# Value chunks of a Gated DeltaNet stage: transposed on TensorE, or by VectorE in 32x32 blocks with a trip through DRAM

## The chip, the cores and the metric

One core of a Trainium2 chip runs the whole kernel. The metric is the time of one execution in device microseconds. The profile is of one execution of its own.

## The reference

The input is 256 tokens of width 1024. Two layers of a first block (windowed attention, gated linear attention and attention into a memory) are followed by two layers of feed-forward, mixer, feed-forward. The mixer of the last layer is the Gated DeltaNet, the stage that is changed:

```
proj = x @ w_in                       # 1024 -> q 1024, k 1024, v 2048, z 2048, beta 16, a 16
qkv  = silu(causal_depthwise_conv(qkv, conv_w))     # width 4, along the tokens, one filter for each channel
q, k = l2norm(q), l2norm(k)           # 8 heads of 128, each used by 2 value heads
o    = chunk_gated_delta_rule(q, k, v, g, beta)     # 16 value heads of 128
o    = rms_norm(o) * norm_w * silu(z)
out  = o @ w_out
```

## The kernel before

The tokens lie in two tiles of 128 (TT = 2). Weights arrive in units of 1 MB in a ring of four slots (SyncE issues the loads), ScalarE rounds each unit to w_hi (steps `hi:n:half`, L209), VectorE forms the rest w_lo (`lo:n:half`, L227), and TensorE multiplies each tile three times (L245 to L247), 24 matmuls of 128x512 for a unit. A unit may start when both halves of its w_lo are there.

In the Gated DeltaNet stage the projection comes in chunks of 512 columns: k0, ba (beta and a), k1, q0, q1, v0 to v3, z0 to z3, of two units each (ba is one small one). The k0 units are numbers 0 and 1; v0 has 9 and 10, v1 11 and 12, v2 13 and 14, v3 15 and 16, z0 17 and 18, z1 19 and 20. What each engine does, and in which order, is written out by hand in GDN_ORDER. Every engine walks the same list and does its own part of each step, so moving a step moves it in the order of each engine that has a part in it; between engines only semaphores order anything. `unit:v1:0:3` is quarter 3 of the first unit of chunk v1.

After a chunk's two units, ScalarE copies the two banks A[0] and A[1] to the chunk buffer u (`evac`, L2557), with the tokens in the partitions. The convolution runs along the tokens, so the channels must be in the partitions. `conv:c:part` does this for half a chunk: TensorE makes four 128x128 transposes from u into bank A[2] or A[3] (L2362), ScalarE writes the last tap's product to t (L2605), and VectorE adds the other three taps with six operations that read the bank (L2781). Steps `silu` follow on both engines, then for k and q `l2` and `norm` (a matmul with ones, L2370), for v `vt` (four transposes back, L2405, and the copy to v). The banks A[2] and A[3] are shared by conv, norm, vt, qk, kk and ba, in the order of the list. Two chunk buffers alternate, and the squares of `z2` go through net.tmp.

Steps `core:g:x` are the delta rule for two value heads. In x2, x1 and x0 a triangular inverse is put together from 16x16 blocks; p0 to p4 apply it. The blocks themselves are inverted on GpSimd (`gather`, function solve, L2191 and L2193), once for the first half and once for the second. SyncE brings them there and back through DRAM: `blocks`, `gather`, `solved` and `spread`, the last with 15 small DMAs that core x2 waits for. GpSimd has nothing else to do in this stage but three loads at its start.

Of the kernel before, what the change touches and what calls it, by code (L numbers as in the profile page):

```python
# [1707 lines left out]
class Conv:  # L1708
# [1403 lines left out]
```

## Time and profile before

| | |
|---|---|
| median of 3 runs | 1417.77 us (1417.53 to 1418.01) |
| the profiled execution | 1416.56 us, span 1414.8 us |
| TensorE busy | 1392.3 us, 98% |
| VectorE busy | 1026.2 us, 73% |
| ScalarE busy | 1011.9 us, 72% |
| GpSimd busy | 68.9 us, 5% |
| DMA queue of SyncE | 233.57 MB, 51.1% of the 16 DMA engines' span |
| DMA queue of GpSimd | 3.35 MB, 0.8% |

The stage runs from about 957 us to about 1224 us of the span. A share over the whole span says little of it: the engines are read stage by stage. A matmul's end is modelled, and the next one starts before it, so on TensorE one reads the distance from one start to the next (about 0.23 us for a 128x512 matmul), and not the durations.

### The profile page before, as it was taken

The numbers are of one execution on the slowest core, as the hardware profiler recorded it, in microseconds if no ns is written. First come the engines' busy times: TensorE is split into PE (matmuls) and PEld (weight loads), VectorE is DVE, ScalarE is ACT, GpSimd is POOL, SyncE is SP. The second block draws the span as 40 slices with busy tenths as digits, with TensorE's granted clock in tenths as the row PEclk, the third lists the DMA queues.
The fourth block names the chain that finished last, engine by engine and source line by source line (L and its number), as shares of the span: only waits on it lengthen the run. The fifth ranks groups of instructions, "written<-read, shape, count | busy, mean of one in ns | idle before, by whom it ended". The sixth has DMA issues, their size and how long they took to land.

```text
span 1414.8 us, 20634 instructions
## 1 busy us (share of the span) xinstructions
PE 1392.3 (98%) x7859; PEld 1142.9 (81%) x7859; DVE 1026.2 (73%) x1417; ACT 1011.9 (72%) x1826; POOL 68.9 (5%) x163
## 2 busy tenths in 40 slices
PE   6999999999999999999999999999999999999998
PEld 5888888888888887788887888887778888788886
DVE  5878788777666766676667766677989886876665
ACT  7657574748777554587875977767888886588784
POOL 8000000000000000000000000001030300000000
PEclk9999999999999999999999999999999999999999
DMA  7542453345656555565655565646453432566562
GB/s 234 166 142 91 145 200 121 119 149 180 201 186 206 180 190 181 158 207 188 205 181 179 195 202 185 203 157 194 129 163 112 118 123 90 165 208 200 187 206 91
DMA packets 168291, 238.27 MB, mean 168 GB/s; under 512 B 21554, under 2 KB 114640, under 8 KB 168192
## 3 DMA queue, kind: packets, MB, share of 16 engines
q1 hardware_dynamic: 166496, 233.57, 51.1%
q0 software_dynamic: 1632, 3.35, 0.8%
q8 instruction: 63, 1.03, 0.3%
q14 instruction: 36, 0.29, 0.1%
q10 hardware_dynamic: 64, 0.02, 0.0%
HBM read 235.07 MB, written 1.84 MB: 167 GB/s over the span
## 4 chain that ended last, share of the span: by engine, by line
PE 93%; ACT 3%; DVE 2%; DMA 1%; issue 1%; SPq 0%; DVEq 0%; ACTq 0%
PE A L245 17%; PE A L246 17%; PE A L247 17%; PE M L247 5%; PE G L246 5%; PE M L246 5%; PE G L247 5%; PE M L245 5%; PE G L245 5%; PE A L1325 1%; PE G L1246 1%; PE G L1293 1%; DVE tmp L414 1%; PE M L1303 1%; ACT w_hi L209 1%; DVE x_lo L419 1%
## 5 line engine op out<-in xcount | busy, mean ns | idle before, releaser
L227 DVE TENSOR_TENSOR w_lo<-raw,w_hi 128x1024 fp32r<-128x1024 f32 (+2 forms) x296 | 506.8, 1726 | 128.7 <-ACT w_hi L209 128.0
L209 ACT ACTIVATE w_hi<-raw 128x1024 fp32r<-128x1024 f32 (+2 forms) x296 | 426.7, 1462 | 120.9 <-DMA raw<-in_ffn_w_gate_up 93.3
L245 PE MATMUL A<-w_hi,x_hi 128*128 128x512 f32 (+1 forms) x640 | 258.7, 404 | 3.6 <-DVE x_lo L419 1.0
L247 PE MATMUL A<-w_hi,x_lo 128*128 128x512 f32 (+1 forms) x640 | 247.1, 386 | 0.0
L246 PE MATMUL A<-w_lo,x_hi 128*128 128x512 f32 (+1 forms) x640 | 246.5, 385 | 0.0
L690 ACT ACTIVATE ffn_ffn_hT<-ffn_ffn_hb 32x128 f32<-32x128 f32 x576 | 176.9, 307 | 15.6 <-DVE ffn_ffn_hb L755 2.5
L245 PEld LDWEIGHTS A<-w_hi,x_hi 128*128 128x128 f32 x640 | 120.2, 188 | 33.5 <-DVE x_lo L419 6.8
L247 PEld LDWEIGHTS A<-w_hi,x_lo 128*128 128x128 f32 x640 | 120.1, 188 | 25.1
L245 PE MATMUL A<-w_hi,ffn_ffn_hT_hi 128*128 128x512 f32 x352 | 139.0, 395 | 0.0
L246 PE MATMUL A<-w_lo,ffn_ffn_hT_hi 128*128 128x512 f32 x352 | 138.4, 393 | 0.0
L246 PEld LDWEIGHTS A<-w_lo,x_hi 128*128 128x128 f32 x640 | 120.5, 188 | 21.0 <-issue 0.7
L247 PE MATMUL A<-w_hi,ffn_ffn_hT_lo 128*128 128x512 f32 x352 | 136.9, 389 | 0.0
L247 PE MATMUL M<-w_hi,x_lo 128*128 128x512 f32 x320 | 124.5, 389 | 0.0
L245 PE MATMUL G<-w_hi,x_hi 128*128 128x512 f32 x320 | 124.5, 389 | 0.0
L246 PE MATMUL G<-w_lo,x_hi 128*128 128x512 f32 x320 | 124.5, 389 | 0.0
L245 PE MATMUL M<-w_hi,x_hi 128*128 128x512 f32 x320 | 124.5, 389 | 0.0
L246 PE MATMUL M<-w_lo,x_hi 128*128 128x512 f32 x320 | 124.5, 389 | 0.0
L247 PE MATMUL G<-w_hi,x_lo 128*128 128x512 f32 x320 | 124.5, 389 | 0.0
L247 PEld LDWEIGHTS A<-w_hi,ffn_ffn_hT_lo 128*128 128x128 f32 x352 | 66.1, 188 | 14.9
L245 PEld LDWEIGHTS A<-w_hi,ffn_ffn_hT_hi 128*128 128x128 f32 x352 | 66.1, 188 | 14.6
L246 PEld LDWEIGHTS A<-w_lo,ffn_ffn_hT_hi 128*128 128x128 f32 x352 | 66.2, 188 | 13.0
L245 PEld LDWEIGHTS G<-w_hi,x_hi 128*128 128x128 f32 x320 | 60.1, 188 | 12.6
(392 smaller groups left out, 2018.5 us busy)
## 6 DMA issues: line engine op xcount, KB each, us to landing
raw<-in_ffn_w_gate_up SPq DMA_DIRECT2D x176, 512.0 KB, 4.8
raw<-in_ffn_w_down SPq DMA_DIRECT2D x88, 512.0 KB, 4.0
raw<-in_w_in SPq DMA_DIRECT2D x48, 512.0 KB, 4.2
raw<-in_gdn_w_in SPq DMA_DIRECT2D x48, 512.0 KB, 4.6
raw<-in_sc_w_in SPq DMA_DIRECT2D x24, 512.0 KB, 4.3
raw<-in_w_out SPq DMA_DIRECT2D x16, 512.0 KB, 4.5
raw<-in_gdn_w_out SPq DMA_DIRECT2D x16, 512.0 KB, 4.0
raw<-in_w_mem_kv SPq DMA_DIRECT2D x8, 512.0 KB, 5.9
```

Of the source, the lines that this page charges most:

```text
L209: ins = act.activation(net.w_hi[:, v % RING, part], net.raw[:, v % RING, part], ACT.Copy)
L227: ins = dve.tensor_tensor(net.w_lo[:, v % RING, part], net.raw[:, v % RING, part], net.w_hi[:, v % RING, part].bitcast(F32), ALU.subtract)
L245: pe.matmul(out, xh, hi[:, k, c, :], start=start and k == 0, stop=False)
L246: pe.matmul(out, xh, lo[:, k, c, :], start=False, stop=False)
L247: mm = pe.matmul(out, xl, hi[:, k, c, :], start=False, stop=stop and k == nk - 1)
L414: dve.tensor_tensor(self.y(n), self.banks[n][:, :].rearrange("p (k t) -> p k t", k=4), self.g[:, 4 * h:4 * h + 4].unsqueeze(2).to_broadcas ...
L419: dve.tensor_tensor(self.part(self.x_lo, n), self.y(n), self.part(self.x_hi, n).bitcast(F32), ALU.subtract).then_inc(self.lo.sem, 1)
L690: ins = act.activation(self.hT[32 * b:32 * b + 32, :, :, i, :].rearrange("p k t n -> p t k n"), self.hb[32 * i:32 * i + 32, :, :, b, :], A ...
L1246: mm = pe.matmul(bank[:, n * P + t * 64:n * P + (t + 1) * 64], self.KE[rows, 1 + lev, tok], right, start=True, stop=True, tile_position=(D ...
L1293: mm = pe.matmul(bank[:, at:at + keys], qT[rows, pair, tt * P:(tt + 1) * P], kT[rows, pair, 0:keys], start=True, stop=True, tile_position= ...
L1303: mm = pe.transpose(bank[:, b * P:(b + 1) * P], self.Pb[:, i % 3, b * P:(b + 1) * P], ident[:, :])
L1325: mm = pe.matmul(O[:, tt * T + at:tt * T + at + HD], pt[:, b * P:(b + 1) * P], v[:, kt, cols], start=(kt == 0), stop=(b == blocks[tt][-1]))
```

## The change

The value chunks v0 to v3 are no longer transposed by TensorE. ScalarE's evac writes them with the columns in another order. In a new step `tb` VectorE transposes the chunk in place in 32x32 blocks, one instruction of 128x1024. GpSimd's queue then writes the 512 KB to DRAM, waits for it, and in step `mv` reads it back with four DMAs, one for each block row; their runs are of 32 floats (128 bytes), 1024 runs for each DMA. The chunk then has its channels in the partitions, in SBUF, and ScalarE and VectorE read it there in place of a bank. A third chunk buffer is made from net.tmp (v0 and v3 use it), and the squares of `z2` go to net.scratch. Where an evac reuses a buffer that held a value chunk, it waits for that chunk's last reader. GDN_ORDER is written anew around this.

```
-    unit:v1:0:1 hi:14:0 solved:0
-    unit:v1:0:2 hi:14:1
-    unit:v1:0:3 silu:q1:0:0 kk:4:0
+    unit:v1:0:1 solved:0
+    unit:v1:0:2 hi:14:0 hi:14:1
+    unit:v1:0:3 tb:v0 mv:v0 evac:v1:0 silu:q1:0:0 kk:4:0
     unit:v1:1:0 lo:13:0
-    unit:v1:1:1 evac:v1:0 spread:0 kk:4:1 lo:13:1
+    unit:v1:1:1 spread:0 kk:4:1 lo:13:1
     unit:v1:1:2 kd:4:0
     unit:v1:1:3 kd:4:1 evac:v1:1
-    unit:v2:0:0 silu:q1:1:0 silu:q1:0:1 l2:q1:0 lo:14:0 kk:5:0
-    unit:v2:0:1 silu:q1:1:1 kk:5:1 kd:5:0
-    unit:v2:0:2 l2:q1:1 kd:5:1 lo:14:1 lo:15:0 lo:15:1 hi:15:0
-    unit:v2:0:3 hi:15:1 norm:q1:0 norm:q1:1
-    unit:v2:1:0 core:0:x2 core:1:x2 core:0:t2 core:1:t2
+    unit:v2:0:0 silu:q1:1:0 silu:q1:0:1 lo:14:0 kk:5:0
+    unit:v2:0:1 tb:v1 silu:q1:1:1 kk:5:1 kd:5:0
+    unit:v2:0:2 l2:q1:0 l2:q1:1 kd:5:1 lo:14:1 lo:15:0 hi:15:0 lo:15:1
+    unit:v2:0:3 mv:v1 hi:15:1 core:1:x2 norm:q1:0 norm:q1:1
+    unit:v2:1:0 core:0:x2 core:0:t2 core:1:t2
...
-    unit:k1:1:3 lo:6:0 hi:6:1 evac:k1:1 norm:k0:0
-    unit:q0:0:0 lo:6:1 l2:k0:1 conv:k1:0
-    unit:q0:0:1 hi:7:0 norm:k0:1 hi:7:1
+    unit:k1:1:3 ba:0 lo:6:0 hi:6:1 norm:k0:0 evac:k1:1
+    unit:q0:0:0 lo:6:1 l2:k0:1
+    unit:q0:0:1 conv:k1:0 hi:7:0 norm:k0:1 hi:7:1
...
-    unit:q1:1:3 lo:9:0 lo:9:1 lo:10:0 lo:10:1 hi:10:1 ba:2 norm:k1:0 blocks:0 norm:k1:1 conv:q0:0 conv:q0:1
+    unit:q1:1:2 l2:k1:1 lo:9:0 lo:9:1 lo:10:0 lo:10:1 hi:10:1 ba:2 norm:k1:0 blocks:0 evac:q1:0
+    unit:q1:1:3 norm:k1:1 conv:q0:0 conv:q0:1
...
+    unit:v3:0:1 silu:v0:0:0 tb:v2 silu:v0:1:0 qk:0
+    unit:v3:0:2 core:1:t1 mv:v2
...
+    unit:z0:0:2 tb:v3
+    unit:z0:0:3 mv:v3 core:0:p4 vt:v1:0
...
+BY_BLOCKS = ("v0", "v1", "v2", "v3")
+U_OF = {"k0": 0, "k1": 1, "q0": 0, "q1": 1, "v0": 2, "v1": 0, "v2": 1, "v3": 2, "z0": 0, "z1": 1, "z2": 0, "z3": 1}
...
+            elif step[0] == "tb":
+                n = self.bys.index(step[1])
+                pool.wait_ge(*self.u_blocks(n + 1))
+                pool.dma_start(self.u_dram[n], self.turned(step[1]).rearrange("p k n -> p (k n)"))\
+                  .then_inc(self.u_out.sem, 16)
+            elif step[0] == "mv":
+                n = self.bys.index(step[1])
+                pool.wait_ge(*self.u_out(16 * (n + 1)))
+                src = self.u_dram[n].rearrange("(i c) (m b n) -> b c m i n", i=4, b=4, n=32)
+                for b in range(4):
+                    pool.dma_start(self.turned(step[1])[32 * b:32 * b + 32, :, :]
+                                 .rearrange("p k (t i n) -> p (k t) i n", t=TT, i=4), src[b]).then_inc(self.u_in.sem, 16)
...
-            elif kind == "conv":
+            elif kind == "conv" and step[1] not in BY_BLOCKS:
                 c, part = step[1], int(step[2])
                 bank = self.take(pe, step)
                 pe.wait_ge(*self.evacuated(2 * self.evacs.index(c) + 2))
...
+            elif kind == "tb":
+                c = step[1]
+                u = self.turned(c).rearrange("p k n -> p (k n)")
+                dve.wait_ge(*self.evacuated(2 * self.evacs.index(c) + 2))
+                dve.transpose(u, u).then_inc(self.u_blocks.sem, 1)
```

The step `conv:v0:0` stays at `unit:v2:1:1`, `conv:v1:0` at `unit:v3:0:3`, `conv:v2:0` at `unit:z0:1:0` and `conv:v3:0` at `unit:z1:0:3`; ScalarE waits there for the data to have landed from DRAM.

## Rows read from the trace of the kernel before

**Rows 1.** The page's busy times, and its chain that ended last, by engine
```profile
PE 1392.3 (98%) x7859; PEld 1142.9 (81%) x7859; DVE 1026.2 (73%) x1417; ACT 1011.9 (72%) x1826; POOL 68.9 (5%) x163
...
PE 93%; ACT 3%; DVE 2%; DMA 1%; issue 1%; SPq 0%; DVEq 0%; ACTq 0%
```

**Rows 2.** Windows of the stage: length, engines' busy times, clock, DMA share, GB/s
```profile
1037.00:1050.00 13.00, 13.00 (x67) 10.86 (x66) 12.01 (x29) 10.29 (x18) 1.30 (x4) 1.00 0.59 129
1050.00:1072.00 22.00, 21.84 (x364) 17.18 (x363) 18.06 (x40) 17.25 (x37) 0.00 (x0) 1.00 0.48 155
1072.00:1112.00 40.00, 40.00 (x468) 34.02 (x467) 36.32 (x84) 33.26 (x75) 3.18 (x5) 1.00 0.40 119
```

**Rows 3.** TensorE's timeline around conv:v0 and conv:v3:1: start, duration, engine, line
```profile
1057.34 0.60 PE L2362 MATMUL A<-ident,gdn_gd_u 128*128 128x128 f32 x4
1057.87 0.69 PE L2476 MATMUL G<-gdn_gd_T,gdn_gd_MT 32*32 32x32 f32 x32
1058.49 0.66 PE L2362 MATMUL A<-ident,gdn_gd_u 128*128 128x128 f32 x4
1058.90 0.47 PE L245 MATMUL A<-w_hi,x_hi 128*128 128x512 f32 x1
1059.22 0.39 PE L246 MATMUL A<-w_lo,x_hi 128*128 128x512 f32 x1
...
1113.07 0.60 PE L2362 MATMUL A<-ident,gdn_gd_u 128*128 128x128 f32 x4
1113.60 1.14 PE L2491 MATMUL G<-gdn_gd_T,gdn_gd_MT 64*64 64x64 f32 x16
```

**Rows 4.** TensorE's timeline at conv:k1:0 and at conv:q0:1
```profile
987.72 0.40 PE L247 MATMUL A<-w_hi,x_lo 128*128 128x512 f32 x1
988.22 0.66 PE L2362 MATMUL A<-ident,gdn_gd_u 128*128 128x128 f32 x4
...
1017.97 0.66 PE L2362 MATMUL A<-ident,gdn_gd_u 128*128 128x128 f32 x4 [0.49 <-ACT gdn_gd_sg L2622]
```

**Rows 5.** VectorE's groups by shape in the stage: busy us, mean ns
```profile
L2781 DVE SCALAR_TENSOR_TENSOR gdn_gd_t<-A,cols,gdn_gd_t 128x254 f32<-128x254 f32 x32 | 13.9, 477 | 0.6
...
L2862 DVE TENSOR_TENSOR gdn_gd_u<-gdn_gd_u,gdn_gd_sg 128x1024 f32<-128x1024 f32 x4 | 4.9, 1218 | 0.0
...
L755 DVE STREAM_TRANSPOSE ffn_ffn_hb<-ffn_ffn_h 128x512 f32<-128x512 f32 x1 | 0.7, 712 | 0.0
```

**Rows 6.** Timeline: lo:14:1, first matmul of unit 14, first value tap
```profile
1049.71 1.22 DVE L227 TENSOR_TENSOR w_lo<-raw,w_hi 128x1024 fp32r<-128x1024 f32 x1
...
1051.99 0.79 PE L245 MATMUL A<-w_hi,x_hi 128*128 128x512 f32 x1
...
1058.00 0.84 ACT L2605 ACTIVATE gdn_gd_t<-A,cols 128x256 f32<-128x256 f32 x2
```

**Rows 7.** GpSimd's DMA instructions by shape (8 rows; 128 rows of 512 bytes)
```profile
L3025 POOL DMA_DIRECT2D rows<-in_norm_g x6 | 3.0, 502 | 0.0
...
L3025 POOL DMA_DIRECT2D rows<-in_gdn_conv_w x1 | 0.6, 556 | 0.0
```

**Rows 8.** DMA issues: count, KB each, median us from issue to landing
```profile
brow<-in_norm_g POOLq DMA_DIRECT2D x6, 512.0 KB, 3.9
...
gdn_gd_MT<-gdn_solved SPq DMA_DIRECT2D x16, 16.0 KB, 2.6
```

**Rows 9.** DMA queue between 1044 and 1050 us: packets, MB, share of 16 engines
```profile
q1 hardware_dynamic: 2365, 0.24, 36.7%
```

**Rows 10.** GpSimd's timeline: one operation of each solve
```profile
1028.00 1.17 POOL L2191 TENSOR_TENSOR gdn_gd_Dpart<-gdn_gd_D,gdn_gd_Dinv 128x64 f32<-128x64 f32 x1
...
1115.69 0.31 POOL L2191 TENSOR_TENSOR gdn_gd_Dpart<-gdn_gd_D,gdn_gd_Dinv 128x64 f32<-128x64 f32 x1
```

**Rows 11.** Timeline: last DMA of the second spread, and core:4:x2 behind it
```profile
1132.66 0.45 SPq L2256 DMA_DIRECT2D gdn_gd_MT<-gdn_solved  x1
...
1137.86 0.73 PE L2457 MATMUL G<-gdn_gd_T,gdn_gd_MT 32*32 32x16 f32 x64
```

More of the change, by code:

```diff
@@ L1970 @@
-    unit:v3:0:1
-    unit:v3:0:2
-    unit:v3:0:3 lo:16:0 core:1:x0 core:0:x0 hi:17:1 silu:v0:0:1 lo:16:1 vt:v0:0 silu:v0:1:1 core:1:t0 lo:17:0 ba:3
+    unit:v2:0:0 silu:q1:1:0 silu:q1:0:1 lo:14:0 kk:5:0
[3 more added lines that the diff above has]
+    unit:v2:1:0 core:0:x2 core:0:t2 core:1:t2
+    unit:v2:1:1 conv:v0:0 core:0:x1 hi:16:0 conv:v0:1 evac:v2:0 core:1:x1 hi:16:1
@@ L1984 @@
+    unit:z0:0:3 mv:v3 core:0:p4 vt:v1:0
+    unit:z0:1:0 vt:v1:1 z2:z0:0 core:1:p4 lo:19:1 conv:v2:0 hi:20:1 core:2:x2
     unit:z0:1:1 conv:v2:1 blocks:1 evac:z0:0
-    unit:z0:1:2 hi:21:0 evac:z0:1
+    unit:z0:1:2 evac:z0:1 hi:21:0
     unit:z0:1:3 hi:21:1 core:3:x2 silu:v2:0:0 core:2:t2
-    unit:z1:0:0
-    unit:z1:0:1 silu:v2:1:0 lo:20:0 silu:v2:0:1
+    unit:z1:0:0 silu:v2:1:0
+    unit:z1:0:1 lo:20:0 silu:v2:0:1
     unit:z1:0:2 core:3:t2
@@ L2022 @@
     out:2:1 lo:28:1
[L2023 to L2024 removed]
+    out:2:2 hi:29:1 hi:30:0 lo:29:0 hi:30:1 core:6:p1 core:7:p1 core:6:p2 core:7:p2
+    out:2:3 z1:z3:0
     out:3:0 core:7:p3 core:6:p3
@@ L2061, in __init__ @@
         self.evacuated = s("evacuated")
+        self.u_blocks, self.u_out, self.u_in, self.u_read = (s(f"u_{n}") for n in ("blocks", "out", "in", "read"))
+        self.u_dram = net.scratch_dram(f"{name}_u", [len(BY_BLOCKS), P, TT * 512])
         self.ba = {x: s(f"ba_{x}") for x in ("act", "dve", "pe")}
@@ L2095, in __init__ @@
         self.silus = [x[1:3] for x in self.steps if x[0] == "silu" and x[3] == "0"]
+        self.bys = [x[1] for x in self.steps if x[0] == "tb"]
+        self.convs = [x[1:3] for x in self.steps if x[0] == "conv" and x[1] in BY_BLOCKS]
         self.norms = [x for x in self.steps if x[0] == "norm"]
@@ L2098, in __init__ @@
         self.l2s = [x[1:3] for x in self.steps if x[0] == "l2"]
-        uses = [x for x in self.steps if x[0] in ("conv", "norm", "vt", "qk", "kk") or
+        uses = [x for x in self.steps if x[0] == "conv" and x[1] not in BY_BLOCKS or x[0] in ("norm", "vt", "qk", "kk") or
                 (x[0] == "ba" and x[1] in "t12") or (x[0] == "ot" and int(x[1]) < 4)]
@@ L2109, in u_of, with turned, conv_read @@
     def u_of(self, c):
-        return self.u[:, [x for x in self.evacs if x != "ba"].index(c) % 2]
+        return self.us[U_OF[c]]
+    def turned(self, c):
+        return self.u_of(c).rearrange("p t c -> p (t c)").rearrange("p (k n) -> p k n", k=4)
+    def conv_read(self, eng, c, part):
+        if c in BY_BLOCKS:
+            eng.wait_ge(*self.u_read(self.convs.index((c, part)) + 1))
+        else:
+            eng.wait_ge(*self.bank_dve[int(part)](self.reads(("conv", c, part))))
     def tensors(self, net):
@@ L2594, in act @@
                 c, part = step[1], int(step[2])
-                bank = self.written(act, step)
+                if c in BY_BLOCKS:
+                    act.wait_ge(*self.u_in(64 * (self.bys.index(c) + 1)))
+                    u = self.turned(c)[:, 2 * part:2 * part + 2, :]
+                else:
+                    u = self.written(act, step)[:, :].rearrange("p (k n) -> p k n", k=2)
                 n = self.silus.index((c, step[2]))
@@ L2793, in dve @@
                 if step[3] == "0":
-                    taps = ("conv",) + step[1:3]
-                    dve.wait_ge(*self.bank_dve[int(step[2])](self.reads(taps)))
+                    self.conv_read(dve, step[1], step[2])
                     if n >= 2 and self.silus[n - 2][0][0] != "v":
```

107 lines of the change are left out of this document (57 added, 50 removed).

## The prediction

> **What bounds the kernel now.** I read the page first: TensorE is busy 98% of the span and holds 93% of the chain that ended last [rows 1]. VectorE's 73% there is a mean over all stages, so I went on to the windows of the stretch that the change touches. There TensorE has next to no idle time, while VectorE is busy 12.01 of 13 us, 18.06 of 22 and 36.32 of 40 [rows 2]. The reader is to see two things. A microsecond taken from TensorE is a microsecond won as long as nothing else is late. And VectorE has only 0.99 + 3.94 + 3.68 = 8.6 us free in these 75, so it is the next bound. The DMA engines are busy 0.40 to 0.59 of the time [rows 2], and GpSimd nearly idle. Last I read the timelines around each step that moves.
>
> **What TensorE loses.** Eight steps conv:v go, four transposes each. The first holds the engine from 1057.34 to 1057.87, 0.53 us. The second from 1058.49 to 1058.90, 0.41 us, and the weight matmul behind it then takes 0.32 us to the next start in place of 0.23, so a change between the two kinds of work costs 0.09. The last one takes 0.53 us [rows 3]. Over the eight, by the same reading, the blocks hold 0.36 to 0.53 us and add up to 3.56 us, with 0.09 more where weight matmuls stand on both sides. Against that, where a conv stood between weights and a core step, the change of kind stays and moves to that step: I give back about 0.1 us at two or three places. The sum is 3.4 us. Its bounds are 8 x 0.36 = 2.9 and 8 x 0.53 = 4.2 us.
>
> **What the new sequence does early.** conv:k1:0 now stands one quarter later, behind norm:k0:0 and unit:q0:0:1, and evac:k1:1 has that much more time. Before, 0.50 us lay between the last matmul and its transposes where 0.23 is usual [rows 4]; that is 0.27 us won. norm:k1:0 moves ahead of unit:q1:1:3, so ScalarE reads the bank of norm:k1:1 without the other norm in front, and conv:q0:1, which waited 0.49 us [rows 4], waits less; I take 0.3 us, between 0 and 0.5. Together 0.6 us.
>
> **What VectorE gains in work.** A block transpose of 128x512 takes 0.712 us, and an operation with one output of 128x1024 takes 1.218 [rows 5]. I take 1.22 us for a tb, between 1.2 and 2 x 0.712 = 1.42. Four are 4.9 us. The 48 tap operations now read SBUF in place of a bank; at 477 ns for 254 elements against 1218/4 = 305 at the least for a quarter of 1024 [rows 5] they could get faster, up to 8 us in all, or stay. The fixed part of so short an operation speaks for staying: I take 0. ScalarE's taps and its evac in another column order I take at 0 too, and ScalarE has 13 - 10.29 = 2.7 us of cover just where evac:v1:0 moves ahead of silu:q1:0:0 and makes it wait for TensorE [rows 2].
>
> **Where that is not hidden.** tb:v0 and tb:v1 both come ahead of lo:14:1 in VectorE's order, and that step ended at 1050.93 for a unit that started at 1051.99 [rows 6]: a margin of 1.06 us. The two add 2.44 us. VectorE's idle time between 1037 and 1050 is 0.99 us [rows 2]; if 0.8 of it absorbs, lo:14:1 ends at 1052.6 and unit 14 waits 0.6 us (bounds 0 and 1.4). Queued behind it on VectorE are lo:15, the norms of q1 and the t2 of core 0 and 1, for which TensorE's x1 waits; the moved conv:v0 has cleared TensorE's way by less than that, and these just meet. From there to unit 20 tb:v2 and tb:v3 follow, and TensorE comes up to 3 us early for the t2 and t1 of core 2 and 3, the vt of v2 and lo:20:1, while VectorE has 7.6 us idle to give [rows 2], much of it waits for TensorE's transposes that now fall away. I take another 0.6 us there, with bounds 0 and 1.8. Sum of stalls 1.2 us.
>
> **The round trip.** tb:v0 can begin where conv:q1 ends on VectorE, about 1039.1, and ends at 1040.3. The write of 512 KB on GpSimd's queue is like the row of brow, 3.9 us from issue to landing [rows 8]: 1044.3. Then four DMAs of 1024 runs. The trace has none of this size on that queue. An issue of 8 rows takes 0.502 us and one of 128 rows 0.556 [rows 7]. By the difference, 0.45 ns for each further run, one of 1024 takes 0.96 us and the four 3.8; in plain proportion it takes 8 x 0.556 = 4.4 and the four 17.8. I take the first, as 16 times the rows cost only a tenth more, and keep both. The transfer: between 1044 and 1050 the packets were mostly 64 byte ones and 2365 of them took 36.7% of 6 us on 16 engines, 14.9 ns each [rows 9]. 4096 of them are 61 us on 16 engines, 3.8 us, much of it beside the issuing. With 2.6 us for the last to land [rows 8] the chunk is there at about 1050.7, and at 1055 if the spread of the first half and two weight units, which fall into this stretch, halve its speed. The first tap stood at 1058.00 [rows 6]. So v0 has 3 to 7 us to spare, and the three later ones 20 us or more from tb to tap. Weight loads meet 1 MB more for each value chunk and 3.8 us of small packets; in the windows they share engines that are half idle [rows 2], and a unit is loaded a few us ahead of its rounding: 0.
>
> The Trainium skill, page "VectorE: DVE Perf Modes", section "The three transpose paths", speaks against this part: a plain DMA that transposes by its access pattern is said to be 19 times slower than the crossbar's when the innermost stride of the destination is large. Here both sides have runs of 32 floats and the elements are turned before, so the sum above stays; by that rule the chunk would come late and the time would be that of the rival "data late". No row here shows such a copy.
>
> The third buffer adds waits of evac v2, v3, z0 and z1 for conv steps that lie ten or more quarters back: 0. The new wait before the squares is for VectorE's own reduction just before: 0.
>
> **The sum.** 3.4 + 0.6 - 1.2 = 2.8 us less. The profiled execution took 1416.56 us (span 1414.8 and 1.8 around it), which is 1.2 under the median; I take the difference over to the median: 1417.77 - 2.8 = 1415.0 us.
>
> **Rivals.** *VectorE has slack for all of it*: the tap operations do get shorter, or its idle time absorbs the four tb whole. Then no stall: 3.4 + 0.6 = 4.0 us less, 1413.8. For it speak 8.6 us of idle for 4.9 us of work, against it that the margin of unit 14 is 1.06 us.
>
> *VectorE becomes the bound*: none of its idle time can be used, because it lies between semaphores. Then 4.9 us of work less the margin of 1.06 comes out on TensorE, 3.8 against 4.0 won: 1417.6. For it speaks that 92% of a window is already full [rows 2].
>
> *Data late*, the one on the other side: GpSimd's descriptors take their time in proportion to runs. A chunk then holds GpSimd's queue for 3.9 + 0.5 + 17.8 = 22.2 us, and four in a row end at 1040.3 + 88.8 + 2.6 = 1131.7, where conv:v3 stood at 1113. ScalarE, whose rounding of weights is queued behind the tap, stops; after some 5 us of units in hand TensorE stops too. 19 - 5 - 4 = 10 us slower: 1428. It decides from the point where the four DMAs together hold the queue for more than 1058 - 1044.3 - 2.6 = 11 us; at 14 us the gain is gone. The Trainium skill, page "SBUF — State Buffer", section "SBUF: two separate sides", gives a way to it: descriptors of GpSimd's DMAs are written through a port pair that VectorE holds in its faster modes. No row here shows it for a DMA.
>
> *The second solve is late*: a GpSimd operation took 1.17 us beside VectorE's w_lo and 0.31 us beside conv:v3 [rows 10]. conv:v3 now has two inputs in SBUF; if each of its twelve operations holds up one of GpSimd's, the solve ends 12 x (0.477 - 0.39) = 1 us later, up to 5 if it is shut out whole. The last DMA of the second spread was issued at 1132.66 and takes 2.6 us, and core:4:x2 came at 1137.86 [rows 11]: 2.6 us of margin. So 0, and at the worst 2.4 us lost: 1417.4. The same page, section "Who interferes with whom", says that a VectorE operation with two SBUF inputs holds up a GpSimd one that reads SBUF; the 1.17 us agree.
>
> **Chances.** The forecast 0.45 (1414.2 to 1416), slack for all 0.18 (1413.2 to 1414.2), VectorE or the solve as bound 0.22 (1416 to 1418.5), data late 0.15 (1419 to 1435). The range: below, the second case with TensorE's upper bound of 4.2, so 1413.0; above, past the third case and into the weaker half of the last, 1419.0. Leaving out all but a tenth at the top and little below holds 8 in 10. 0.2% is 2.8 us, about what measurement tells from none, and the forecast lies on that line: its half and the second case make faster 0.42; its other half and most of the third same 0.42; slower 0.16.
>
> **What would show it.** Right: no L2362 with a value chunk and 32 fewer of them, TensorE's idle in the stage under 2 us, four block transposes of about 1.22 us, the reads landed by 1055 for v0, GpSimd's four issues about 1 us each. Wrong: issues of several us; ScalarE's tap idle for a DMA; TensorE idle ahead of unit 14 or of x1 and t1 for VectorE by more than 2 us in all; weights (L209) waiting for DMA; the second solve ending after core:4:x2 is due. The forecast fails most likely through VectorE's order, next through GpSimd's queue.

## The result: slower by 0.38%, outside the range

The changed kernel takes 1422.29 us (median of 9 runs, 1420.18 to 1425.88), the kernel before, run beside it, 1417.53 (9 runs, 1416.38 to 1418.14). The ratio is 1.0038, interval 1.0029 to 1.0047. I had forecast 1415.0 and given 0.16 to "slower". The profiled execution of after took 1421.78 us, its span 1420.0.

**The page of after**, busy times and the chain by engine:

```profile
PE 1392.2 (98%) x7827; PEld 1141.7 (80%) x7827; DVE 1032.3 (73%) x1421; ACT 1012.1 (71%) x1826; POOL 90.9 (6%) x183
...
PE 87%; DVE 3%; DMA 2%; POOL 2%; ACT 2%; SPq 1%; issue 1%; DVEq 0%; ACTq 0%; POOLq 0%
```

TensorE has its 32 matmuls fewer, as planned. VectorE has 6.1 us more work, where 4.9 was planned. TensorE's share of the chain fell from 93 to 87% [rows 1]; GpSimd and SP's queue stand in it now, and DMA has 2% for 1%: the chain runs over transfers.

**Windows of after**, laid 1.8 us later, as the stage starts that much later. Columns as in [rows 2]:

```profile
1038.80:1051.80 13.00, 13.00 (x66) 10.78 (x65) 12.48 (x25) 8.61 (x16) 5.54 (x10) 1.00 0.73 182
1051.80:1073.80 22.00, 19.99 (x333) 14.75 (x333) 18.97 (x44) 17.39 (x36) 5.26 (x8) 1.00 0.76 228
1073.80:1113.80 40.00, 39.19 (x469) 33.17 (x468) 39.16 (x87) 34.38 (x75) 10.49 (x13) 1.00 0.64 163
```

TensorE is idle 2.0 us of the middle window, where it was 0.16 before, and the DMA engines' share is 0.76 where it was 0.48 [rows 2].

**What TensorE waited for**, 957 to 1250 us, after (line, releaser, us in total, times, longest):

```profile
PE G L2487 <- DMA gdn_gd_MT<-gdn_solved: 3.3, 2, 1.7
PE M L2499 <- issue: 1.1, 1, 1.1
PE A L280 <- ACT gdn_gd_u L2596: 0.8, 1, 0.8
PE G L2506 <- DVE gdn_gd_T L2964: 0.6, 1, 0.6
```

L2487 is step x2, the first to read a spread's matrices. It waits twice, once for each spread; before, it never did. L2499 is the second half of t2 and waits for no semaphore ("issue"). L280 was there before. VectorE, which I had feared, stands fourth.

**TensorE's timeline of after** at both spreads and in t2 (the bracket is the idle time before, and what ended it):

```profile
1054.24 0.44 PE L2487 MATMUL G<-gdn_gd_T,gdn_gd_MT 32*32 32x16 f32 x32 [1.57 <-DMA gdn_gd_MT<-gdn_solved]
...
1141.52 0.73 PE L2487 MATMUL G<-gdn_gd_T,gdn_gd_MT 32*32 32x16 f32 x64 [1.73 <-DMA gdn_gd_MT<-gdn_solved]
...
1145.37 0.23 PE L2499 MATMUL M<-gdn_gd_MT,gdn_gd_X 32*16 32x16 f32 x9
1146.72 0.32 PE L2499 MATMUL M<-gdn_gd_MT,gdn_gd_X 32*16 32x16 f32 x21 [1.12 <-issue]
```

core:4:x2 comes at 1141.52, where it came at 1137.86 [rows 11]. The last row shows a step broken in two: nine matmuls, 1.12 us of nothing, twenty-one more.

**The second solve and what follows it, after**: GpSimd's reads of v3, its first and last operation, SP's last transfer of the spread:

```profile
1104.63 4.02 POOL L2231 DMA_DIRECT2D tmp<-gdn_u  x4 [6.24 <-DMA gdn_u<-tmp]
...
1112.28 0.39 POOL L2209 TENSOR_TENSOR gdn_gd_Dpart<-gdn_gd_D,gdn_gd_Dinv 128x15 f32<-128x15 f32 x1 [2.94 <-DMA gdn_gd_D<-gdn_blocks]
...
1129.57 1.50 POOL L2216 COPY gdn_gd_D<-gdn_gd_Dinv 128x256 f32<-128x256 f32 x1
...
1139.62 0.45 SPq L2286 DMA_DIRECT2D gdn_gd_MT<-gdn_solved  x1
```

The last transfer is issued 7.0 us later than before [rows 11]. In the trace of before the solve began at 1108.51 and ended with its copy at 1124.05; here it is 1112.28 and 1131.07. So 3.8 us are a late start and 3.2 a longer solve, 1.8 of the former being the later start of the stage.

**When the matrices land and when they are wanted.** I subtract from each time the start of the stage (TensorE's first wait of 0.78 us, at 969.59 before and 971.36 after). The last matrix of the first spread then lands at 80.3 us before and 82.8 after, and the step that reads it is due at 84.3 before; in the new order it is due at 81.2 (e1, where it waits for nothing). So the transfer lands 2.5 us later and its reader comes 3.1 us sooner. The last matrix of the second spread lands at 164.8 before and 170.1 after. Its own transfer is as quick as ever (1.75 and 1.85 us); what is late there is the solve.

**How I compare the stage.** The offset between two executions at entry is not the stage's doing, so I take the *stage time*: from matmul 1300 to matmul 1500 of L245, counted from 0 (1012.17 to 1229.24 before). It is 217.1 us before and 220.2 after. Summed start to start by kind of matmul, the transposes of `gdn_gd_u` in it fall from 5.82 to 1.98 us. So 3.84 us came off and 3.1 + 3.84 = 6.9 came on. Of the 3.84, 3.55 are the value chunks; the other 0.29 is a shorter wait of conv:q0:1. The stage time is of one profiled execution of each kernel, and after and after again differ by 0.4 us in it.

### The profile page after: what moved, and what is told of

Its sections match the earlier page's. It is cut to its first block, busy times and chain, and to the rows that moved or that the text cites. A ratio compares the mean times of both kernels' runs of the same rounds, so it can differ in the third digit from the quotient of the medians.

```text
span 1420.0 us, 20597 instructions
## 1 busy us (share of the span) xinstructions
PE 1392.2 (98%) x7827; PEld 1141.7 (80%) x7827; DVE 1032.3 (73%) x1421; ACT 1012.1 (71%) x1826; POOL 90.9 (6%) x183
## 4 chain that ended last, share of the span: by engine, by line
PE 87%; DVE 3%; DMA 2%; POOL 2%; ACT 2%; SPq 1%; issue 1%; DVEq 0%; ACTq 0%; POOLq 0%
PE A L245 16%; PE A L246 15%; PE A L247 15%; PE M L245 5%; PE M L247 5%; PE G L246 5%; PE G L245 5%; PE G L247 5%; PE M L246 5%; PE A L1325 1%; POOL gdn_gd_Dinv L2211 1%; PE G L1246 1%; POOL gdn_gd_Dpart L2209 1%; DMA gdn_gd_D<-gdn_blocks 1%; PE G L1293 1%
## 5 line engine op out<-in xcount | busy, mean ns | idle before, releaser
L245 PE MATMUL A<-w_hi,x_hi 128*128 128x512 f32 (+1 forms) x640 | 259.6, 406 | 3.5 <-DVE x_lo L419 1.2
L245 PEld LDWEIGHTS A<-w_hi,x_hi 128*128 128x128 f32 x640 | 120.7, 189 | 33.7 <-DVE x_lo L419 6.8
L245 PE MATMUL A<-w_hi,ffn_ffn_hT_hi 128*128 128x512 f32 x352 | 139.1, 395 | 0.0
L245 PE MATMUL G<-w_hi,x_hi 128*128 128x512 f32 x320 | 124.5, 389 | 0.0
L245 PE MATMUL M<-w_hi,x_hi 128*128 128x512 f32 x320 | 124.5, 389 | 0.0
L245 PEld LDWEIGHTS A<-w_hi,ffn_ffn_hT_hi 128*128 128x128 f32 x352 | 66.1, 188 | 14.3
L245 PEld LDWEIGHTS G<-w_hi,x_hi 128*128 128x128 f32 x320 | 60.1, 188 | 12.6
```

What stands on the lines that cost most here:

```text
L245: pe.matmul(out, xh, hi[:, k, c, :], start=start and k == 0, stop=False)
```

## The experiments

Medians are compared by ratio, as chips differ (the kernel before ran at 1417.1 to 1418.8 beside these). The granted clock is the share of full speed that TensorE was given. "Clock" is what the stage lost to one under 1.00: (1 - clock) times the length, summed over its windows. Taking it off is an estimate, right as far as TensorE was busy meanwhile.

| kernel | median us | ratio (95%) | stage us | of it clock |
|---|---|---|---|---|
| before | 1417.5 | 1 | 217.1 | 0 |
| after | 1422.3 | 1.0038 (1.0029-1.0047) | 220.2 | 0 |
| after again (e14) | 1423.8 | 1.0042 (1.0027-1.0058) | 220.6 | 0 |
| e1 new order, TensorE turns all | 1419.8 | 1.0012 (1.0003-1.0022) | 219.2 | 0 |
| e2 old order, four turned | 1421.7 | 1.0011 (0.9997-1.0025) | 221.1 | 1.7 |
| e3 after without its transfers | 1416.8 | 0.9989 (0.9980-0.9999) | 215.6 | 0 |
| e4 after, v3 by TensorE | 1419.7 | 1.0015 (1.0005-1.0025) | 219.9 | 1.7 |
| e17 after, v0 by TensorE | 1421.3 | 1.0020 (1.0011-1.0030) | 221.1 | 1.7 |
| e10 after, v0 and v3 by TensorE | 1418.4 | 1.0004 (0.9996-1.0013) | 217.0 | 0 |
| e9 after without block transposes | 1423.2 | 1.0036 (1.0024-1.0048) | 222.0 | 3.4 |
| e5 core:1:x2 back | 1422.4 | 1.0034 (1.0023-1.0045) | 221.2 | 1.7 |
| e6 cores 4, 5 later | 1425.1 | 1.0051 (1.0039-1.0063) | 224.4 | 3.4 |
| e7 both | 1429.0 | 1.0074 (1.0061-1.0086) | 227.0 | 8.5 |
| e11 old order, v1 late, v2 | 1422.8 | 1.0037 (1.0023-1.0051) | 221.1 | 1.7 |
| e12 the same and v0 | 1421.8 | 1.0032 (1.0019-1.0045) | 219.9 | 1.7 |
| e15 old order, v1 early, v2 | 1416.2 | 0.9983 (0.9975-0.9992) | 214.9 | 0 |
| e19 the same and v0 | 1416.1 | 0.9985 (0.9977-0.9994) | 216.1 | 0 |
| e20 the same and v0, v3 | 1419.5 | 1.0008 (0.9999-1.0017) | 218.7 | 1.7 |
| e16 stream moved by 256 | 1426.0 | 1.0052 (1.0039-1.0064) | 228.2 | 5.1 |
| e18 stream moved by 128 | 1425.0 | 1.0051 (1.0038-1.0063) | 222.5 | 1.7 |

### The order, the turning and the transfers apart: e1, e2, e3, e9

```diff
 e1: -BY_BLOCKS = ("v0", "v1", "v2", "v3")     +BY_BLOCKS = ()       (no tb, no mv)
 e2: the order of before, with tb:v0 mv:v0 at v1:0:0, v1 at v1:1:3, v2 at v2:1:2, v3 at z0:0:2
 e3: -act.wait_ge(*self.u_in(...))             +act.wait_ge(*self.u_blocks(n + 1))    (no write, no reads)
 e9: no dve.transpose; pool.wait_ge(*self.evacuated(...)) before the write
```

e3 leaves the values between blocks unturned and e9 the values inside them, so their outputs are not the reference's.

> The new sequence of steps and the three chunk buffers alone: TensorE transposes the value chunks as before, no block transposes and no trip to DRAM. Theory A (the time goes into two waits of TensorE for the spreads of the solved blocks, because the second solve starts late and runs long and because core:1:x2 was moved ahead): without the DMAs of the chunks and with the taps read from a bank the solve takes 15.5 us again and both spreads land in time, so about 1417.5, within 1 of the kernel before. Rival B (VectorE has become the bound): also near 1417.5, since its 4.9 us are gone. Rival C (the new sequence itself is the loss, whatever turns the chunks): 1420 or more.

> The old sequence of steps, with block transposes and the trip to DRAM put in right behind each value chunk's evac. Theory A: core:1:x2 stands where it stood and waits less, by about 1.5 us; the second spread is as late as in the changed kernel; 1420 to 1421. Rival B: VectorE's order is not fitted to the 4.9 us, TensorE waits for it in many places, 1423 or more. Rival C: 1418 or less, as the loss was in the sequence.

> The changed kernel without the writes and reads of the chunks: VectorE transposes the 32x32 blocks, and the taps read them as they lie, so blocks stay out of place and the values are not the reference's. VectorE and ScalarE do all that they do in the changed kernel. Theory A: the first wait (about 1.8 us) goes, blocks and gather of the second half are not held up (about 3 us of 7), the solve stays long: 1417 to 1419. Rival B: the DMAs cost nothing, 1421 to 1422. Rival C: 1421 to 1422.

> The changed kernel without the four block transposes of VectorE (the values of v are then not the reference's); writes, reads and their waits stay and start 1.2 us earlier. Theory A (the DMA round trip and its effect on the spreads and the second solve are the loss): within 0.7 us of the changed kernel, 1421.5, with the gaps at core:1:x2 and core:4:x2 still over 1.2 us each. Rival B (VectorE's 4.9 us are the loss): 2 us or more faster than the changed kernel, and the two gaps small.

e1: the order alone is no gain; it costs 2.1 us of stage, with TensorE turning the values. By kind of matmul it is spread: 0.7 us behind weight matmuls, 0.6 at x1 and x2, 0.5 at the transposes of v, 0.4 at the products of v, less 0.3 won at the norms. It had been written for a kernel whose values VectorE turns.

e3: without the transfers, VectorE's four block transposes and the new order included, the stage is 215.6 us, 4.6 below after and 3.6 below e1. The value transposes that e1 has and e3 has not hold TensorE for 3.8 us, so VectorE's 4.9 us of added work cost about 0.2. The stage thus adds up: 2.1 for the order, 3.6 off for turning on VectorE, 4.6 for the transfers, 3.1 in all. No x2 waits in e3. Its waits of TensorE, first and third row:

```profile
PE A L280 <- ACT gdn_gd_u L2584: 0.8, 1, 0.8
...
PE M L2487 <- issue: 0.6, 1, 0.6
```

e9 is the mirror of it: transfers without VectorE's 4.9 us. By its median it is as slow as after; less the clock its stage is 222.0 - 3.4 = 218.6 us, so that VectorE's transposes account for 1.6 us at most. In e2 core:1:x2 does not wait, core:4:x2 waits 1.75 us, and t2 and t1 stall; less the clock its stage is 219.4. Its ten runs go from 1415.5 to 1422.8 us, four of them below the median of the kernel before, 1418.7 beside it, so one profile says little of it.

### Which chunk: e4, e17, e10

```diff
 e4:  BY_BLOCKS = ("v0", "v1", "v2")     e17: BY_BLOCKS = ("v1", "v2", "v3")     e10: BY_BLOCKS = ("v1", "v2")
```

> The changed kernel with chunk v3 alone given back to TensorE: eight transposes more (about 0.9 us), and the taps of v3, which run beside the second solve, read a bank again; no chunk DMAs in the stretch of the second blocks and gather. Theory A: the second solve takes 15.5 us in place of 18.8 and starts 1 to 3 us sooner, TensorE's wait ahead of core:4:x2 is gone or under 1 us: 1418 to 1419.5. Rival B: 1.2 us less for VectorE against 0.9 more for TensorE: 1421.5 to 1422.5. Rival C: 1422 to 1423.

> The changed kernel with v0 turned by TensorE again (its round trip left out), v1 to v3 by VectorE. Theory D: the wait at core:1:x2 (1.94 and 1.95 us in the two profiles) goes or falls under 0.8 us; the second solve is still stretched to 17 to 19 us by v3's products out of SBUF, but starts 2 us earlier, so that the wait at core:4:x2 is under 1 us; 1419 to 1420, between the changed kernel (1422.3) and the one with v1 and v2 alone (1418.4). If the two sources only add, without the second depending on the first: the wait at core:4:x2 stays at 2 us or more, and 1420.5 or more.

> The changed kernel's order, with v1 and v2 by VectorE and the round trip, v0 and v3 by TensorE. In the window in which the first spread lands only v1's round trip is left; no value chunk is in SBUF form while the second solve runs on GpSimd. Theory D (the loss is the sum of the waits at the spreads, a TensorE instruction fetch that lands late behind data, and in some executions a fall of TensorE's granted clock behind such a wait, all of them set off by the DMA load and the stretched solve): second solve 15.5 us, no wait over 0.6 us at core:4:x2, but the wait at core:1:x2 (1 to 2.5 us) stays, 1419 to 1420. Rival (VectorE's added work is the loss, in proportion): half of the changed kernel's loss of 4.8 us, 1420.5, spread over the stage and not in single gaps.

e4 has no wait at core:4:x2, but 1.9 us at core:1:x2. e17 has none at core:1:x2, but 1.8 us at core:4:x2 and 1.4 us in t2. e10 has neither. That is what each chunk does in the new order. v0's write and reads (issued 1042 to 1052) share the engines with the first spread. With v0 turned by VectorE the last matrix lands 82.8 to 83.1 us into the stage (after, e4), without it at 79.9 to 80.3 (e3, e10, e17, and before). v3 makes the second solve late. The second wait does not need the first; there "they only add" came true, against what I expected of e17. e10 stands 1.4 us of stage above e3 and has four conv steps more on TensorE, which hold it for 2.1.

### The old order with two, three and four chunks: e11, e12, e15, e19, e20

```diff
 e11: order of before; tb:v1 mv:v1 at v2:1:1 (behind core:1:x1), tb:v2 mv:v2 at v3:0:1; v0 and v3 by TensorE
 e12: and tb:v0 mv:v0 at v1:0:0
 e15: as e11, tb:v1 mv:v1 at v2:0:1
 e19: as e15, and tb:v0 mv:v0 at v1:0:0
 e20: as e19, and tb:v3 mv:v3 at z0:0:2
```

> The order of the kernel before, with v1 and v2 by VectorE and the round trip: v1's starts only behind core:1:x1 (about 1057), when the first spread has landed, v2's at unit v3:0:1; v0 and v3 by TensorE. Theory D: no wait at either spread, second solve 15.5 us, clock 1.00 throughout; four conv steps of 0.43 us (the 3.4 us of eight, halved: 1.7 us) come off TensorE, 1416.0 to 1417.0, faster than before by 0.1%. Rival (VectorE's 2.5 us of transposes reach TensorE through the products that it turns late): 1418 or more.

> As the one with v1 and v2, and v0 by VectorE and the round trip too, started at unit v1:0:0, so that it should have landed before the first spread's transfers are issued (about 1046 in the kernel before); v3 by TensorE. Theory D: six conv steps, 2.6 us, come off TensorE: 1415.2 to 1416.5. If v0's traffic still delays the first solve's transfers (written and read back between 1044 and 1050): a wait of 1 to 2.5 us at core:0:x2 and 1418 or more. Rival (VectorE): 1419 or more.

> The order of the kernel before; v1 and v2 by VectorE and the round trip, v1's now started at unit v2:0:1 (the run that started it behind core:1:x1 had its data 4 us late), v2's at v3:0:1; v0 and v3 by TensorE. Theory D: no wait for v1's data, none at the spreads, 1.9 us of transposes come off TensorE: 1416.0 to 1417.0 where the kernel before has 1417.5, and no stretch of the granted clock under 1.00 in the stage. Rival (VectorE's and ScalarE's work is what TensorE waits for): 1418.5 or more, with waits for VectorE of together 2 us.

> The order of the kernel before with v0, v1 and v2 by VectorE and the round trip (v0's started at unit v1:0:0, v1's at v2:0:1, v2's at v3:0:1) and v3 by TensorE: against the kernel with v1 and v2 alone (1416.15, stage 214.9) two more transposing steps go, 0.9 us. If v0's transfers, between 1040 and 1053, do not reach the first spread's (issued 1040 to 1048): 1415.0 to 1415.6. If they do: a wait of 0.5 us or more at core:0:x2, or a fetch stall near 1060, and 1416.5 or more.

> The same with v3 too, so that all that differs from the changed kernel is the order and the start of the transfers. v3's products out of SBUF stretch the second solve from 15.5 to 17 to 19 us (copy 1.50 us for 0.63), the second spread lands about 2.5 us later, and core:4:x2, which had 2.6 us to spare in the kernel before, waits 0.5 to 2 us; with it a fetch stall of about 1 us can come: 1416 to 1418.5, and 1 to 3 us above the kernel with three. If the second solve is not what costs, it is 0.9 us below it.

e11 and e12 missed through my placing: in e11 v1 was turned from 1065.9 on, and VectorE later stood idle for 4.4 us, until 1081.15, for ScalarE's tap of the data that had not landed. TensorE, e11:

```profile
PE M L2542 <- DVE gdn_gd_S L2985: 4.0, 1, 4.0
```

With v1 moved two quarters ahead (e15) every wait but those of before is gone, and the stage takes 214.9 us, 2.2 less than before, for four convs removed. It is faster than the kernel before, 0.17%.

e19 adds v0 and gains nothing: by medians it equals e15, its stage is 1.2 us longer although v0's two conv steps (0.9 us) are gone. Three waits for VectorE are new, 0.5 us at the values' transposes, 0.4 at a norm and 0.7 at the start of the output. The first spread is not spared either. Its last matrix lands 83.6 us into the stage, 3.3 later than before; but its first reader is due at 84.9 there, so nothing waits. In the new order it is due at 81.2. The first wait of after thus takes two things, v0's transfers and the reader moved ahead: with the transfers alone (e2, e5, e7, e12, e19, e20) or the move alone (e1, e3, e10, e17) it does not occur.

e20 adds v3 and loses 3.3 us of median and 2.6 of stage, of which 1.7 is the clock. Less the clock it takes 0.9 us longer than e19 for 0.9 us of transposes less, so v3 itself costs 1.8. All four chunks in the old order stand 0.08% above the kernel before, which is not clear of noise, where in the new order they lose 0.38%: by stage less the clock 217.0 us against 220.2, with another start of the transfers too. The pair e19, e20 differs in v3 alone, so here its price is read. GpSimd's groups in the second solve (busy us, mean ns), and its start, its end and the x2 behind it; first both of e19, then of e20:

```profile
L2211 POOL TENSOR_TENSOR gdn_gd_Dinv<-gdn_gd_Dinv,gdn_gd_Dpart 128x15 f32<-128x15 f32 (+7 forms) x15 | 6.6, 439 | 1.2
L2209 POOL TENSOR_TENSOR gdn_gd_Dpart<-gdn_gd_D,gdn_gd_Dinv 128x15 f32<-128x15 f32 (+7 forms) x15 | 5.9, 392 | 28.3 <-DMA gdn_gd_D<-gdn_blocks 27.2
```

```profile
1106.80 0.21 POOL L2209 TENSOR_TENSOR gdn_gd_Dpart<-gdn_gd_D,gdn_gd_Dinv 128x15 f32<-128x15 f32 x1 [27.16 <-DMA gdn_gd_D<-gdn_blocks]
1121.60 0.62 POOL L2216 COPY gdn_gd_D<-gdn_gd_Dinv 128x256 f32<-128x256 f32 x1
1136.40 0.73 PE L2487 MATMUL G<-gdn_gd_T,gdn_gd_MT 32*32 32x16 f32 x64
```

```profile
L2211 POOL TENSOR_TENSOR gdn_gd_Dinv<-gdn_gd_Dinv,gdn_gd_Dpart 128x15 f32<-128x15 f32 (+7 forms) x15 | 7.6, 507 | 1.2
L2209 POOL TENSOR_TENSOR gdn_gd_Dpart<-gdn_gd_D,gdn_gd_Dinv 128x15 f32<-128x15 f32 (+7 forms) x15 | 7.3, 486 | 5.3 <-DMA gdn_gd_D<-gdn_blocks 4.2
```

```profile
1110.98 0.27 POOL L2209 TENSOR_TENSOR gdn_gd_Dpart<-gdn_gd_D,gdn_gd_Dinv 128x15 f32<-128x15 f32 x1 [4.20 <-DMA gdn_gd_D<-gdn_blocks]
1128.22 0.62 POOL L2216 COPY gdn_gd_D<-gdn_gd_Dinv 128x256 f32<-128x256 f32 x1
1139.34 1.05 PE L2487 MATMUL G<-gdn_gd_T,gdn_gd_MT 32*32 32x16 f32 x64 [2.12 <-DMA gdn_gd_MT<-gdn_solved]
```

The same 30 operations take 14.9 us in place of 12.5. About 1.0 of it is what they lose beside conv:v3, which now reads both inputs in SBUF: e3, without transfers, has 13.4 against 12.4 in e1. The other 1.4 are two operations of about 0.3 us that took 1.17, six over 0.9 us in place of four. In after these are

```profile
1121.78 1.17 POOL L2209 TENSOR_TENSOR gdn_gd_Dpart<-gdn_gd_D,gdn_gd_Dinv 128x60 f32<-128x60 f32 x1
1123.03 1.17 POOL L2211 TENSOR_TENSOR gdn_gd_Dinv<-gdn_gd_Dinv,gdn_gd_Dpart 128x60 f32<-128x60 f32 x1
```

and VectorE runs two w_lo operations beside them, from 1121.46 to 1124.03. The solve also starts 4.2 us later, 1.4 of it the offset at entry: the gather that feeds it was issued at 1102.88 and landed 8.0 us later (e19: 1101.00 and 5.7 us), because v3's four reads went out at 1102 to 1105, the very time of the gather.

### Moving the reader: e5, e6, e7

```diff
-    unit:v2:0:3 mv:v1 hi:15:1 core:1:x2 norm:q1:0 norm:q1:1       (e5, e7)
-    unit:v2:1:0 core:0:x2 core:0:t2 core:1:t2
+    unit:v2:0:3 mv:v1 hi:15:1 norm:q1:0 norm:q1:1
+    unit:v2:1:0 core:0:x2 core:1:x2 core:0:t2 core:1:t2
-    unit:z2:1:2 ... core:4:x2 core:5:x2 vt:v3:0 vt:v3:1            (e6, e7; t2 to p0 of both cores follow)
+    unit:z2:1:3 z2:z0:2 core:4:x2 core:5:x2 evac:z2:0 z1:z1:0
```

> The changed kernel with one step moved back to its old place: core:1:x2, the first TensorE step that reads the first spread matrices, stands behind norm:q1 and unit v2:1:0 again. Theory A (each spread lands late and TensorE waits at its first reader): the gap of 1.95 us at 1054.24 is covered by the two norms and the unit (about 2.5 us), so the kernel is 1.5 to 1.9 us faster than the changed one, near 1420.6, with the gap of 2.12 us at core:4:x2 still there. Rival B (the time is kept by something else, VectorE or ScalarE, and the gap at this step only shows where): another gap of 1 us or more opens within the next 30 us, and the time stays at 1422. Rival C (what the first gap costs is given back before the second, whose start is set by the second solve on GpSimd): the first gap goes, that at core:4:x2 grows from 2.1 to 3.5 us or more, and the time stays at 1422.

> The changed kernel with the steps of cores 4 and 5 up to p0 moved about one quarter unit (1.75 us) later, and core:4:x2 behind vt:v3. Theory A: the gap of 2.12 us before core:4:x2 and the one of 1.29 us at t2 behind it go or fall below 0.5 us each; 2 to 2.5 us faster than the changed kernel, near 1420. Rival B (VectorE or ScalarE keep the pace there): other gaps take their place, 1422. Rival C (the later steps of cores 4 and 5 delay cores 6 and 7 or the output's rows): gaps of together 2 us behind 1160, and 1422 or more.

> Both moves at once. Theory A: both gaps go and about 3.5 to 4 us of the changed kernel's time: near 1418.3, within 1 us of the kernel before; if the 2.7 us that the prediction counted as TensorE work taken away are then to be had in full, 1416. Rival (what is won is lost again behind, to VectorE's 4.9 us or to the longer second solve): 1421 to 1422.

The waits at x2 that were aimed at did go (0.4 us is left at core:4:x2 in e5), yet no kernel gained. In e5 and e7 a fetch stall (explained under e14, below) took the place of the first, 2.2 and 2.5 us inside the t2 of cores 0 and 1. In e6 the stall in t2 stayed (1.6 us), and the moved steps met waits for ScalarE of 2.6 and 1.0 us; in e7 they met 1.6 us for ScalarE in two and 0.8 for VectorE. Behind them the granted clock fell. Windows of e7: length, TensorE busy, clock, DMA share, GB/s:

```profile
1150.00:1155.00 5.00, 3.60 (x43) 0.89 0.00 0
1155.00:1160.00 5.00, 5.00 (x70) 0.50 0.02 3
1160.00:1165.00 5.00, 4.92 (x24) 0.50 0.31 88
1165.00:1170.00 5.00, 5.00 (x26) 0.74 0.30 122
1170.00:1175.00 5.00, 5.00 (x32) 1.00 0.00 0
```

0.50 is 1.2 GHz, the lower of the two levels. These four windows lose 5 x (0.11 + 0.50 + 0.50 + 0.26) = 6.9 us. Less the clock, e7's stage is 218.5 us, 1.7 below after, where I had expected 3.5 to 4. The clock took five times as much as was won.

### Again, and the fetch: e14, e16, e18

```diff
 e16, in x2:
-            for n in range(4):
+            for n in [m for m in range(4) for _ in range(5 if g == 2 else 1)]:
 e18:
+            for n in [m for m in range(4) for _ in range(2 if g in (2, 3) else 1)]:
```

> The changed kernel once more, unedited, for a second profile. If the wait at the first read of each spread and the fetch stall at t2 belong to the program and not to one execution, they stand here too, each within 1 us of its size before; the clock may fall behind one of them, and then the time of that execution is 1424 or more rather than 1422. Theory of chance: the gaps stand in other places.

> The changed kernel with the 16 small products of core:2:x2 issued five times over (64 matmuls more, same values), which moves everything behind them by 128 instructions of TensorE's stream and costs about 0.7 us itself. If the stall inside t2 of cores 4 and 5 is the fetch of the next 256 instructions, it goes from that place (1.29 and 1.78 us in the two profiles of the changed kernel) and no stall of over 0.5 us takes its place, and the time is 0.6 to 1.1 us under the changed kernel's. If it is a wait for ScalarE's or VectorE's result, it stays at t2 with its size, and the time is 0.7 us above the changed kernel's.

> The changed kernel with the small products of core:2:x2 and core:3:x2 issued twice (64 matmuls more in all, same values, 0.7 us), which moves what is behind them by 128 instructions of TensorE's stream, half of the 256 after which each stall stood so far. If the stall inside t2 of cores 4 and 5 is the fetch of the next block, it is gone from that place (1.3 to 1.8 us in every profile with this program's phase, the one moved by 256 too), or stands half a block away, where TensorE reads only large products, under 0.3 us: stage time 0.6 to 1.1 us under the changed kernel's 220.2 to 220.6. If it is a wait for a result, it stays at t2 with its size and the stage is 0.7 us longer.

e14 repeats after to the place: x2 waits for the spreads 3.6 us in two, t2 1.6 us for "issue". These gaps belong to the program. Its profiled execution saw the clock at 1.00 throughout; its span of 1418.3 us is after's 1420.0 less the 1.7 which after lost to a clock of 0.92 and 0.91 between 70 and 90 us, long before the stage. So after is 1418.3 - 1414.8 = 3.5 us slower with the clock left out. The medians are 4.8 apart. I put the 1.3 between them down to the clock, as after's runs have a mean of 0.996 to 0.998 in all but one; no profile was taken of those runs, so that is not shown.

The stall in t2: I counted TensorE's records (matmuls and weight loads) from the start of each trace up to it. After, e14, e3, e6, e9 and e17: 12737. e2: 10945 and 12737. e5: 10689 and 12737. e7: 10689. These are 49, 42 and 41 times 256, plus 193 each time. The trace also holds the transfers of a queue named "instruction", 16 KB each, as many as TensorE's 16005 records have blocks of 256 (62); the kernel before has 63 for 16077. In after the one of this block began at 1144.49 and took 0.93 us; TensorE went on 1.3 us after its end.

A boundary is a record whose number is a multiple of 256 plus 193. The twenty profiles hold 1224 of them, the first of each trace left out. At 15 the packet had ended less than 0.7 us before the block ran out, or only after it, and just these 15 have a gap of over 0.6 us in TensorE's work. At all others it had ended about 1 us or more before, and no gap is over 0.4. From that packet's end to the next record it is 1.2 to 1.6 us. So it is instruction fetch. Why the packet is late is shown less well. It began 2.6 us after the last boundary in after, in before 0.2 us ahead of it. The queues between 1141 and 1145 in after, and below between 1137 and 1141 in before:

```profile
q1 hardware_dynamic: 317, 1.05, 75.1%
q8 instruction: 1, 0.02, 1.5%
```

```profile
q1 hardware_dynamic: 67, 0.21, 13.2%
q8 instruction: 1, 0.02, 1.4%
```

Here SP had just sent off two weight loads behind the late spread, and I take it that the fetch had its turn among their packets. The chunks' own transfers are not needed for it: e3, which has none, stalls 0.6 us at the same boundary, with the queue's share at 62.3%.

e16 did not do what I wrote: a product in f32 is two matmuls and two loads, so the stream moved by 256, a whole block, not by 128. The stall then has to stay, and it did, 1.63 us at the same instruction. The 128 added matmuls also ran a block down so fast that a new one opened, again at 45 times 256 plus 193:

```profile
1101.83 1.23 PE L2487 MATMUL G<-gdn_gd_T,gdn_gd_MT 32*32 32x16 f32 x126
1106.08 0.40 PE L2487 MATMUL G<-gdn_gd_T,gdn_gd_MT 32*32 32x16 f32 x26 [3.02 <-issue]
```

e18 moved it by 128, and t2 of cores 4 and 5 ran through. A boundary still fell into it, but its block had lasted 11.5 us in place of 3.6. A stall of 0.84 us stood at the next one that short products reach (53 times 256 plus 193). The place was right; the time was not: core:4:x2, still short of its matrices, waited 2.7 us, and the clock fell to 0.79 behind it.

The Trainium skill, page "Runtime: NRT & Kernel Launch", section "Instruction fetch mechanics", says that instructions come in blocks of 16 KB, 256 of them, through a DMA queue of the sequencer's own, and that crossing a boundary is mostly hidden. The 16 KB and the 256 agree with these traces; hidden it was at all but 15 of 1224 boundaries, and not at those whose packet came late. The blocks before them had lasted 1.1 to 6.6 us.

## Why the prediction was wrong

**TensorE's loss of work**, 3.4 us: right; 3.55 measured for the value chunks, inside 2.9 to 4.2.

**The new sequence early**, 0.6 us won: wrong, and the second step that failed. conv:q0:1 did wait less (0.25 us for 0.49), and the norms won 0.3. But the offset between after and before, 1.8 us from 775 us on, grew to 2.1 at 1000 and was back at 1.8 at 1032 (e14: -0.3, 0.0, -0.3), so up to there nothing was won in all. And the sum gives no price to any other moved step, where the order alone costs 2.1 us of stage (e1). I had costed the two moves beside which I saw a wait, and none of the others.

**VectorE**, 1.2 us of stalls: too much. Block transposes took 1.23 us, tap operations 477 to 494 ns from SBUF for 477 from a bank, so 0 was right for them. Unit 14 did not wait; x1 of cores 2 and 3 did, 0.6 us. In all e1 and e3 leave about 0.2 us. The rivals that made VectorE the bound are out in the new order; in the old one VectorE does cost: the three new waits in e19 are 1.6 us.

**The round trip**: GpSimd's four issues took 3.9 to 4.0 us (3.8 forecast), but the write took 5.9 us to landing (3.9 forecast) and the reads 5.6 to 6.1, as medians; single ones took 2.9 to 8.9. v0's last read landed at 1058.46, past the 1055 that I had named as a sign of being right, and 3.6 us before its tap, which came at 1062.06. "Data late" did not occur for the chunks of after. The packets were not small either: the four chunks added 1344 of them for 4.2 MB, 3.1 KB each, where I had counted 4096 for one chunk's reads. The Trainium skill gives a factor of 19 (page "VectorE: DVE Perf Modes", section "The three transpose paths") for a copy that transposes by strides and has a large innermost stride at its destination. The copies here had runs of 128 bytes on both sides and landed 128 KB in about 6 us; no run here tests the factor.

**"Weight loads meet 1 MB more for each value chunk ... 0"**: the step that failed. I put the transfers at nothing in the sum; they cost 4.6 us (e3 against after). I asked whether weights and chunks would come in time and not what else crosses those engines. The first spread did, in 15 transfers of 16 KB with TensorE waiting directly behind; the gather of the second solve did. The waits of after are 1.6 us at core:1:x2, 1.7 at core:4:x2 and 1.1 in t2, those of e3 none, none and 0.6. Moving core:1:x2 ahead, which I passed over, took 3 of the 4.0 us of cover that the kernel before had there.

**"The second solve is late"**, 0 with 2.4 at worst: the mechanism was right and named; its size was not. The 1 us beside conv:v3 came out as forecast (e1, e3). But I assumed that the solve starts on time, and that nothing else in it grows. Two more operations fell beside w_lo (1.4 us), the copy grew by up to 0.9, and the start came 2 to 3 us later, with blocks and gather. The margin was 3.5 us, not 2.6, as that last transfer landed in 1.75 us; but TensorE, spared its transposes, also comes sooner to core:4:x2, by 1.9 us in e3, which has 0.5 us left. What the Trainium skill says, page "SBUF — State Buffer", section "Who interferes with whom", agrees with these traces: a solve's 30 operations take 12.4 us in e1 and 13.4 in e3, where conv:v3 reads two inputs in SBUF.

By terms of the sum, forecast and measured in the stage: TensorE's work and VectorE's stalls together 2.2 us off, 3.6 off; the sequence 0.6 off, 2.1 on; the transfers 0, 4.6 on.

What stays open: how the new order's 2.1 us divide over its moves, why the fetch packet is late, and how much of the medians' difference is the clock. Doing the turning's transfers from another queue than GpSimd's was not tried.

## What to carry to other kernels

When a change adds transfers, list everything that uses the DMA engines in those microseconds and has a reader waiting directly behind it, small scattered transfers first. For each, write down when it lands and when its reader is due, and do not move a reader ahead without that number. Half idle engines in a window's mean say nothing of that. Put such transfers into stretches where none of these runs, or leave the reader its cover. Here the two middle chunks alone, in the old order, won 0.17%; all four in that order lost 0.08%, which is not clear of noise, and all four in the new order lost 0.38%. An order fitted to one kernel is a cost of its own for another and is to be timed alone.

## What I had not expected of the hardware

**A wait can cost more than its length.** In 12 of the 20 profiles the granted clock fell in the stage, 15 times in all, 14 of them at or behind a wait of TensorE of 1.6 to 4.0 us. The longest fall, in e7, stood behind three waits of 1.0, 0.8 and 0.6 us. In the kernels whose waits in the stage were all under 0.8 us (before, e1, e3, e10, e15, e19) it never fell. It cost 1.7 us in eight of them, twice that in two (e6, e9), three and five times that in e16 and e7. In after and e14, waits of 1.6 to 2.1 us were spared it, in these executions. Of after's nine runs the fastest (1420.18) has a mean clock of 1.000, all others 0.996 to 0.998.

**TensorE can outrun its own instructions**: in after a block of 256 records was used up in 3.6 us; the next landed just then, and 1.3 us more went by until it ran. A block that lands 1 us or more before it is needed costs at most 0.4 us.

**SBUF operands of VectorE slow GpSimd even where it is not shut out**: in after, operations of the solve beside conv:v3 with 60 to 64 elements took 0.37 to 0.45 us, where one of 64 took 0.31 [rows 10]. Beside a w_lo operation of 128x1024 they took 1.17.
